# A first unit's high half shared by two engines, its products regrouped, and ten filler records in place of 32, in a decoder trunk

## The reference

```python
z = x @ w_in                      # 1024 -> 1952 columns, four head groups
y = concat([spatial_gating(za), latent_attention(zb), gated_conv(zc), pooling(zd)])
h = y @ w_out                     # then cross-attention, then 16 routed experts
```

## Time and profile before

| | |
|---|---|
| median of 3 runs | 732.71 us (732.43 to 732.93) |
| profiled execution | 733.11 us, of which the span of the trace is 731.3 us |
| busy share of the span | TensorE 96%, VectorE 55%, ScalarE 36%, GpSimd 6% |
| mean granted TensorE clock | 0.985 of full speed |
| transfers | 176 MB, 241 GB/s on average |

### The profile page before, as it was taken

One profiled execution on the slowest core, in us unless ns is written; L12 is line 12 of the kernel. 1 busy time (PEld: TensorE's weight loads), 2 busy tenths in 40 slices (PEclk: granted clock), 3 DMA queues, 4 the chain that ended last, 5 costly groups with the idle time before them and its releaser, 6 DMA issues.

```text
span 731.3 us, 11970 instructions
## 1 busy us (share of the span) xinstructions
PE 704.1 (96%) x4792; PEld 566.6 (77%) x4792; DVE 405.6 (55%) x709; ACT 266.2 (36%) x457; POOL 47.2 (6%) x85
## 2 busy tenths in 40 slices
PE   7999999999999999999799999999999999999992
PEld 7979887889988875556399798888898897655541
DVE  5795886674457622121568588848556574211126
ACT  3555743455533131111324565434555132311120
POOL 2700000010003300000111000000000000000001
PEclk9999999999999999999989999999999999999996
DMA  8992344573357799999975323455723595999961
GB/s 282 333 371 73 108 139 173 172 230 117 115 196 297 250 380 396 414 418 411 329 277 171 116 70 118 160 173 181 231 107 116 192 383 221 352 420 417 417 244 61
DMA packets 62495, 176.10 MB, mean 241 GB/s; under 512 B 3824, under 2 KB 37024, under 8 KB 53216
## 3 DMA queue, kind: packets, MB, share of 16 engines
q1 hardware_dynamic: 58112, 161.95, 60.1%
q0 software_dynamic: 4032, 12.24, 5.1%
q10 hardware_dynamic: 288, 1.05, 0.4%
HBM read 174.18 MB, written 1.05 MB: 240 GB/s over the span
## 4 chain that ended last, share of the span: by engine, by line
PE 89%; DVE 6%; DVEq 2%; DMA 1%; issue 1%; ACT 0%; ACTq 0%; POOL 0%
PE ring L2027 15%; PE ring L2062 8%; PE ring L1592 8%; PE ring L1593 7%; PE ring L1594 7%; PE quad L1592 7%; PE quad L1593 7%; PE quad L1594 6%; PE quad L2074 4%; PE ring L1634 3%; PE ring L1891 2%; PE ring L1858 2%; PE quad L1952 2%; PE ring L1653 1%; PE ring L1760 1%; DMA X<-in_x 1%
## 5 line engine op out<-in xcount | busy, mean ns | idle before, releaser
L961 DVE TENSOR_TENSOR w_lo<-raw,w_hi 128x1024 fp32r<-128x1024 f32 x108 | 127.8, 1222 | 42.6 <-ACT w_hi L662 34.4
L662 ACT CAST w_hi<-raw 128x1024 fp32r<-128x1024 f32 x108 | 108.0, 1049 | 65.0 <-PE quad L1594 60.2
L1592 PE MATMUL ring<-x_hi,w_hi 128*128 128x256 f32 x320 | 93.6, 293 | 0.9 <-ACTq L705 0.7
L1594 PE MATMUL ring<-x_hi,w_lo 128*128 128x256 f32 x320 | 91.2, 285 | 0.0
L1593 PE MATMUL ring<-x_lo,w_hi 128*128 128x256 f32 x320 | 91.2, 285 | 0.0
L685 ACT ACTIVATE arena<-ring 128x512 f32<-128x512 f32 (+1 forms) x66 | 35.6, 573 | 85.9 <-PE ring L1594 67.0
L1592 PEld LDWEIGHTS ring<-x_hi,w_hi 128*128 128x128 f32 x320 | 62.0, 194 | 2.3 <-issue 1.9
L1593 PEld LDWEIGHTS ring<-x_lo,w_hi 128*128 128x128 f32 x320 | 62.1, 194 | 0.7 <-issue 0.5
L1510 DVE TENSOR_TENSOR y_lo<-ring,y_hi 128x512 fp32r<-128x512 f32 x32 | 22.1, 692 | 72.9 <-ACT y_hi L915 72.9
L1594 PEld LDWEIGHTS ring<-x_hi,w_lo 128*128 128x128 f32 x320 | 62.0, 194 | 0.0
L2027 PE MATMUL ring<-raw,x_slots 128*64 128x256 f32 x448 | 51.3, 380 | 0.0
(11 more groups left out here) (308 smaller groups left out, 1392.4 us busy)
## 6 DMA issues: line engine op xcount, KB each, us to landing
raw<-in_moe_w_gate SPq DMA_DIRECT2D x20, 1024.0 KB, 6.9
raw<-in_moe_w_up SPq DMA_DIRECT2D x16, 1024.0 KB, 7.7
w_raw<-in_moe_w_up SPq DMA_DIRECT2D x16, 1024.0 KB, 9.4
w_raw<-in_moe_w_down SPq DMA_DIRECT2D x16, 1024.0 KB, 11.1
raw<-in_w_in SPq DMA_DIRECT2D x14, 1024.0 KB, 11.5
raw<-in_moe_w_down SPq DMA_DIRECT2D x12, 1024.0 KB, 10.3
raw<-in_w_out SPq DMA_DIRECT2D x10, 1024.0 KB, 5.0
raw<-in_xattn_wk SPq DMA_DIRECT2D x8, 1024.0 KB, 6.6
```

The source lines that it names most:

```text
L662: nc.scalar.copy(unit_slot(u, 0, n)[:, s], raw[:, SLOT[u], s]).then_inc(hi_done, 1)
L961: low = nc.vector.tensor_tensor(unit_slot(u, 1, n)[:, s], raw[:, SLOT[u], s], unit_slot(u, 0, n)[:, s].bitcast(F32), ALU.subtract)
L1592: mm(out, a_hi, b_hi, start=first, stop=False)
L1594: return mm(out, a_lo, b_hi, start=False, stop=last)
```

## The change

ScalarE's order at the start of layer 0 becomes: `x_high` of x's first tile, the first half of unit 0's high part, `x_high` of the second tile; the second half of unit 0's high part is made by VectorE, between `x_low` of the first tile and `x_low` of the second, and ScalarE counts it in once a new semaphore says so. `first_unit` takes each of its three groups of terms through both column halves before the next; its waits for `x_lo` and for the split now stand ahead of the second and third group. Layer 0's second filler is 5 products (10 records) in place of 16 (32 records).

```diff
+        first_high = sem("first_high")
...
-            def x_high(name, l, x_hi=x_hi):
-
-                for j in range(4):
+            def x_high(name, l, x_hi=x_hi, banks=range(4)):
+
+                for j in banks:
...
                 if l == 0:
-                    x_high("xa", l)
-                    hi(0, l, NORMAL)
+                    x_high("xa", l, banks=range(2))
+                    hi_half(0, l, NORMAL, 0)
+                    x_high("xa", l, banks=range(2, 4))
+                    act.wait_ge(first_high, 1)
+                    act.sem_inc(hi_done, 1)
                     hi_rotary(l)
...
                 if l == 0:
-                    x_low("xa", l, 0)
+                    def second_half_high():
+
+                        dve.wait_ge(raw_full[SLOT[0]], landed(0, 0))
+                        nc.vector.tensor_copy(unit_slot(0, 0, NORMAL)[:, NORMAL // 2:],
+                                              raw[:, SLOT[0], NORMAL // 2:]).then_inc(first_high, 1)
+
+                    x_low("xa", l, 0, second_half_high)
                     lo(0, l, NORMAL)
...
                 o = free("cq", l)
-                for c in range(2):
-                    out_c, cols = o[:, c * SEQ:(c + 1) * SEQ], slice(c * P, (c + 1) * P)
-                    for k in range(DC):
-                        mm(out_c, h[:, k, cols], x_hi[:, k, :], start=k == 0, stop=False)
-                    if c == 0:
+                terms = ((h, x_hi), (h, x_lo), (lw, x_hi))
+                for i, (w, part) in enumerate(terms):
+                    if i == 1:
                         pe.wait_ge(dve_emptied, emptied("xa3", l))
-                    for k in range(DC):
-                        mm(out_c, h[:, k, cols], x_lo[:, k, :], start=False, stop=False)
-                    if c == 0:
+                    elif i == 2:
                         pe.wait_ge(split_done, split(0, l))
-                    for k in range(DC):
-                        r = mm(out_c, lw[:, k, cols], x_hi[:, k, :], start=False, stop=k == DC - 1)
+                    for c in range(2):
+                        for k in range(DC):
+                            r = mm(o[:, c * SEQ:(c + 1) * SEQ], w[:, k, c * P:(c + 1) * P], part[:, k, :],
+                                   start=i == 0 and c == 0 and k == 0, stop=i == 2 and k == DC - 1, skip_group_check=True)
                 r.then_inc(unit_used, 1)
...
-                keep_busy("cq", l, 6 if l else 16)
+                keep_busy("cq", l, 6 if l else 5)
```

## The result

The changed kernel takes 733.77 us (median of 20 runs, 731.99 to 735.43), the kernel before 732.80 in the same comparison (20 runs, 732.20 to 733.63). The ratio is 1.0013, with a 95% interval of 1.0007 to 1.0018: 0.1% slower, and with a wider spread. The forecast was 732.7 with a range up to 733.7, so the median lies just above the range, and it moved up where next to no change was forecast.

What follows compares the result with a forecast made beforehand. TensorE, busy 96%, was taken as bound by VectorE's chain at v and the small weights' landing at the queries, absorbing the 1.9 us gain; profiled 733.11 less 0.05, standing 0.4 above the median, gave 732.7 us, range 731.7 to 733.7.

Steps and rivals of the forecast that it cites:

- TensorE's start, ScalarE, VectorE up to v: Layer 0's start: first unit at 10.8 us, VectorE's low part of unit 2 ending at 23.75, v at some 23.8.
- 0.44 us of slack at v: VectorE's low part of unit 2 ends at 23.49, TensorE loads v's first weights at 23.93; no more slack than that.
- a gain of 1.9 us: Layer 0's first unit starts at 10.8 in place of 12.71; 0.1 to 0.2 us of it left at v.
- edits at nothing: Edits priced at no cost, among them layer 1's first unit, starting when its 12-record filler ends at 372.50: 0.
- The pin on the queries: Queries load at 45.81, pinned through VectorE's cn by the small weights' landing at 36.87; can move by 0.05 at most.
- my own sign of being wrong (queries before 45.5): Layer 0's queries: the forecast counts as wrong if they start before 45.5 us.
- The gain didn't come through: Rival at v and the queries: both covers softer than read, the 1.9 us stay, 730.8 us; chance 6%.
- no half-clock stretch between 10 and 32 us: Rival in layer 0: new idle pieces make TensorE's clock fall, price 1.7 us on v, 734.2 us; chance 6%.
- the second of my signs of being wrong: TensorE's clock in layer 0: the forecast is wrong if it is at half anywhere between 10 and 33 us.
- The stretch forecast for 33.1 to 36.5: TensorE's clock in layer 0: at half from 33.1 to 36.5 us, as before the change.
- The weights of unit 0 landed by 8.8: Rival at layer 0's start: landing forecast at 8.56; at 10.2, v and queries 1.4 us late, 734.1 us; chance 4%.

Runs made afterwards that it cites:

- run 10: The kernel before with 11 of 32 broadcast products left out of layer 0's branch that is not taken: median 734.15 us against 732.79, ratio 1.0018.
- run 9: The changed kernel plus 11 identity products in layer 0's branch that is not taken: median 731.75 us against 732.79, ratio 0.9982.
- run 13: The changed kernel plus 11 identity products in layer 0's untaken branch, measured again in another comparison: median 732.69 us, ratio 0.9990.
- run 11: The kernel before with VectorE's wait for the small weights moved to ahead of their first use: median 730.85 us against 732.79, ratio 0.9976.
- run 18: The kernel before with VectorE's wait for the small weights moved to their first use, measured again: 730.39 us against 732.94, ratio 0.9969.
- run 1: The changed kernel unaltered, measured and traced again: median 734.83 us, ratio 1.0019; span of its trace 732.1 us.
- run 7: The changed kernel unaltered, one more trace: a single execution of 733.73 us, span 732.0 us.
- run 3: The changed kernel plus 6 filler products (12 records) between the ckv and v units of layer 0: median 732.59 us, ratio 0.9996.

## Why the prediction was wrong

**TensorE's start, ScalarE, VectorE up to v: right**, each within 0.2 us in the trace of the changed kernel. In its other traces v starts at 23.71 to 24.14. The reading that VectorE's unbroken chain has 0.44 us of slack at v carried the main point: a gain of 1.9 us on the engine that is busy 96% of the time is worth 0.15 three steps later.

**The step that failed** is the one under "edits at nothing": "that filler stays at 12 records, and the regrouped terms are the same 48 products, so 0". Layer 1's filler does stay at 12 records, but it is no longer run in one piece. I priced the cut of 22 records by their time alone, and not by their place in TensorE's program. A row of the trace of before could have warned me, the idle time of 3.97 us marked `<-issue` ahead of that filler: a standstill for which no engine is to blame, behind a jump. It cost nothing there since VectorE finished x later still, at 366.1; the second stop of 2.1 to 2.8 us pushed the transposes past that point. Cutting the branch measured it at 1.36 us in the kernel before (run 10). Padding it took the changed kernel from 0.97 us above before to 1.04 and 0.21 below it (runs 9 and 13), and the two pairs of traces differ by 1.8 and 1.1 us of span. So the stop is at least the whole loss of 0.97; the rest of it was offset by what the change itself may gain. No term of mine had either.

The Trainium skill, "Runtime: NRT & Kernel Launch", section "Instruction fetch mechanics", says that instructions are refilled in blocks of 16 KiB and that a taken branch to a block that isn't held must wait for a transfer. The trace agrees on both: 42 transfers of 0.69 MB in all are 16.4 KB each, and the first stop stands where the code has the jump, for 4 us, with one such transfer inside it. The same section says that the cost of crossing a block boundary is mostly hidden; right behind a jump it wasn't in the 8 traces with the second stop (2.1 to 2.8 us). That the transfer itself is what TensorE waits for is inferred from the layout, the count and the times of the transfers; the trace names no releaser.

**The pin on the queries: right in mechanism, mis-sized.** I took the landing of the small weights, 36.87, as fixed. It took 7.8 to 8.0 us in 7 of the 20 traces and 9.1 to 9.5 in 13, whatever the kernel, so VectorE resumed anywhere from 35.3 to 37.8. That is a term of a microsecond and more that the forecast had at 0.05, and it makes my own sign of being wrong (queries before 45.5) come true in 3 of the 6 traces of the changed kernel. The landing has both sizes in kernels with and without the change, so it adds spread and doesn't explain the loss. Why it has two sizes stays open. Runs 11 and 18 confirm that this wait is on the path.

**The rivals.** The gain didn't come through. Once the clock had risen, no half-clock stretch between 10 and 32 us appeared in any trace of the changed kernel. But in run 1 it rose only at 12.2: the 10 filler records took 2.34 us in place of 1.28, and the first unit started at 11.79 and not at 10.72, a case that neither the forecast nor its rivals had; v absorbed it (23.84). So the second of my signs of being wrong, half clock between 10 and 33 us, came true in this trace too. The stretch forecast for 33.1 to 36.5 came in 2 of the 6 traces (runs 1 and 7), and not in the first. The weights of unit 0 landed by 8.8 in every trace of the changed kernel. The rival that decided was none of mine. **The range** was too narrow at the top because the second stop was priced at zero.

Left open: what the executions above 735 us look like, since none was caught in a trace. A late landing and the second stop together give run 1 a span 0.8 us above that of the kernel before (732.1 against 731.3), not 2.5.

## What to carry to other kernels

Removing instructions moves all that lies behind them. Where a program jumps, look for idle time marked `<-issue` behind the jump, compare the count of instruction transfers of the two pages, and test with products placed in a branch that isn't taken before blaming clock or overlap. And before pulling an engine forward, look for the next wait that a transfer alone sets: moving such a wait down to its first use was worth 1.9 to 2.6 us here, as much as all that the change set out to win (1.9).

## What was not expected of the hardware

TensorE starts an execution at half rate, and the granted-clock column doesn't say so. In all 20 traces the first 10 filler records take 2.47 or 2.48 us, and 10 of them at full rate take 1.28. TensorE's timeline of run 3, in which the trace's first entry on the clock is a rise at 12.4 us:

```profile
5.18 1.92 PE L1663 MATMUL ring<-ident,X 128*128 128x128 f32 x8
8.58 1.97 PE L1663 MATMUL ring<-ident,X 128*128 128x128 f32 x8 [1.49 <-DMA X<-in_x]
```

The 8 transposes at 8.58 take 1.97 us, the same 8 took 1.15 in the kernel before, while the column reads 1.00 in both. In layer 1 they take 1.97 at a granted clock of 0.50. So rates at the start of a trace are to be read from the length of the records.
